# Four-layer diffusion transformer on one core: convolution taps dealt by head, and 32 modulation units of the third layer placed elsewhere

## The reference, cut to what matters

```
mod_x = silu(c) @ w_ada[i] + b_ada[i]          # 6 x 1024: shift1, scale1, gate1, shift2, scale2, gate2
```

```
s = q . k * scale (two maps per head) ;  p = softmax(s)
w = p[0] - lam * p[1] ;  attn = rmsnorm(w @ v)
z = a * sigmoid(g)                              # 512 channels
z = depthwise_conv(z, 31 taps) + b_dw ;  y_conv = silu(layernorm(z)) @ w_conv_out
out = (sigmoid(g1) * y_conv + sigmoid(g2) * (attn @ w_attn_out)) @ w_out
```

## Time and profile before

| | us |
|---|---|
| median of three runs | 2333.69 |
| lowest, highest | 2329.54, 2333.79 |
| the profiled execution's own time | 2330.94 |
| its span, first to last instruction | 2329.1 |
| TensorE busy | 2247.1 (96%) |
| VectorE busy | 1544.8 (66%) |
| ScalarE busy | 1082.7 (46%) |

### The profile page before, as it was taken

The page is one execution under the profiler, slowest core; times in us unless marked ns, Lnnn a source line. Parts: engine busy times, 40 slices in busy tenths (PEclk is TensorE's granted clock), DMA queues, the critical chain, the costliest instruction groups (busy, mean ns, idle before and its releaser), DMA issues.

```text
span 2329.1 us, 34905 instructions
## 1 busy us (share of the span) xinstructions
PE 2247.1 (96%) x13410; PEld 1869.9 (80%) x13410; DVE 1544.8 (66%) x2639; ACT 1082.7 (46%) x2070; POOL 33.4 (1%) x40
## 2 busy tenths in 40 slices
PE   8999999999899999989999999999999999989999
PEld 6658878888857898877777888888788887888988
DVE  5454777575656767578884455766754788767776
ACT  4453422223545555555566524422323765675543
POOL 0300000000100000000000000000000000000000
PEclk9999999999899999999999999999999999999999
DMA  8452467554365555311112232346652222254554
GB/s 315 159 191 73 154 213 268 178 181 135 107 238 181 195 179 174 105 58 61 46 55 73 75 116 73 138 157 212 216 182 91 91 91 75 80 163 148 192 185 138
DMA packets 95316, 335.44 MB, mean 144 GB/s; under 512 B 10672, under 2 KB 12848, under 8 KB 95024
## 3 DMA queue, kind: packets, MB, share of 16 engines
q1 hardware_dynamic: 95152, 333.21, 42.4%
HBM read 332.12 MB, written 1.05 MB: 143 GB/s over the span
## 4 chain that ended last, share of the span: by engine, by line
PE 81%; DVE 10%; ACT 5%; issue 3%; DMA 1%; SPq 0%; ACTq 0%; DVEq 0%
PE out L1507 19%; PE out L1509 19%; PE out L1508 19%; PE out L1501 7%; PE out L1505 3%; DVE w_lo L1909 2%; DVE stage L2270 2%; PE sc L1573 1%; PE pt L1582 1%; ACT w_hi L1639 1%; PE out L1434 1%; DMA raw<-stream 1%; ACT e_t L1802 1%; PE aux L1394 1%; PE pv L1598 1%
## 5 line engine op out<-in xcount | busy, mean ns | idle before, releaser
L1507 PE MATMUL out<-act,w_lo 128*128 128x512 f32 (+1 forms) x1816 | 648.4, 357 | 8.7 <-DVE w_lo L1909 2.9
L1639 ACT CAST w_hi<-raw 128x1024 fp32r<-128x1024 f32 (+2 forms) x444 | 453.8, 1024 | 431.3 <-PE out L1509 268.8
L1509 PE MATMUL out<-act,w_hi 128*128 128x512 f32 (+1 forms) x1816 | 637.4, 351 | 0.0
L1508 PE MATMUL out<-act,w_hi 128*128 128x512 f32 (+1 forms) x1816 | 637.0, 351 | 0.0
L1909 DVE TENSOR_TENSOR w_lo<-raw,w_hi 128x1024 fp32r<-128x1024 f32 (+2 forms) x444 | 528.3, 1192 | 123.0 <-ACT w_hi L1639 122.2
L1507 PEld LDWEIGHTS out<-act,w_lo 128*128 128x128 f32 x1816 | 345.2, 190 | 64.2 <-issue 12.9
L1509 PEld LDWEIGHTS out<-act,w_hi 128*128 128x128 f32 x1816 | 344.6, 190 | 45.9
L1508 PEld LDWEIGHTS out<-act,w_hi 128*128 128x128 f32 x1816 | 345.1, 190 | 43.5 <-issue 0.2
L1507 PE MATMUL out<-mix,w_lo 128*128 128x512 f32 (+1 forms) x734 | 261.5, 356 | 3.2 <-DVE mix L1931 2.2
L1508 PE MATMUL out<-mix,w_hi 128*128 128x512 f32 (+1 forms) x734 | 260.2, 354 | 0.0
L1509 PE MATMUL out<-mix,w_hi 128*128 128x512 f32 (+1 forms) x734 | 260.1, 354 | 0.0
(11 more groups left out here) (291 smaller groups left out, 2844.9 us busy)
## 6 DMA issues: line engine op xcount, KB each, us to landing
raw<-stream SPq DMA_DIRECT2D x604, 512.0 KB, 3.6
raw<-stream SPq DMA_DIRECT2D x16, 384.0 KB, 3.1
raw<-stream SPq DMA_DIRECT2D x16, 256.0 KB, 2.7
x<-xin SPq DMA_DIRECT2D x4, 512.0 KB, 5.3
consts<-const SPq DMA_DIRECT2D x1, 1088.0 KB, 7.1
x<-ctx SPq DMA_DIRECT2D x1, 1024.0 KB, 6.0
out<-x SPq DMA_DIRECT2D x8, 128.0 KB, 1.7
vecs<-vec SPq DMA_DIRECT2D x1, 287.0 KB, 9.0
```

The lines of the kernel that those rows point to most:

```text
L1507: nc.tensor.matmul(ps, wl, xh, start=(k == 0), stop=False)
L1508: nc.tensor.matmul(ps, wh, xl, start=False, stop=False)
L1509: ins = nc.tensor.matmul(ps, wh, xh, start=False, stop=(k == s.nk - 1))
L1639: nc.scalar.copy(w_hi[:, number % HL, 0:n], raw[:, place[number] % RAW, 0:n]).then_inc(S["hi_ready"], 1)
```

## The change

Three edits. The taps: `k_made` and `q_done` hold one tap each instead of three, and `taps_due` deals 24, 24, 6, 6, 6, 6, 6 to heads 0 to 6, evenly over a head's groups, and all that is left to head 7, in both the third and the fourth layer. The units: bank 1 of the third layer joins the first layer's network as `product`; bank 2 becomes 16 `ada` units in the third layer's mixer from head 2 on, one at the end of each group, in the bank `pt1`; the second layer's mixer has none. The last step of such a unit turns its result through a part of `stage` (`ada_turn`) instead of `k_t`.

```
-UNITS_IN = (1, 2, 2, 2, 2, 2)
+TAPS_IN = (24, 24, 6, 6, 6, 6, 6)
...
-        def taps_due(slots, head):
-
-            left = 4 * CONV_K - sum(taps_done) - 2 * 3 * max(0, 6 - head)
-            return max(0, -(-left // slots))
+        def taps_due(head, part, parts):
+
+            if head == 7:
+                return -(-(4 * CONV_K - sum(taps_done)) // (parts - part))
+            share = TAPS_IN[head]
+            return (part + 1) * share // parts - part * share // parts
...
-                qk_turn(held["k", h], lambda: conv_taps(3))
+                qk_turn(held["k", h], lambda: conv_taps(1))
...
-                held["qr", h] = query_finish(held["q", h], lambda: conv_taps(3))
+                held["qr", h] = query_finish(held["q", h], lambda: conv_taps(1))
...
             for j, g in enumerate(groups):
-                slots = (8 - h) * len(groups) - j
-                g.append(lambda slots=slots, h=h: conv_taps(taps_due(slots, h)))
-                for _ in range(UNITS_IN[j] if ada_left else 0):
-                    unit = ada_left.pop(0)
-                    g.append(lambda a=unit: ada(*a, psum="pt"))
-                    if unit[2:] == (1, KD - 1) or not ada_left:
-                        break
+                g.append(lambda h=h, j=j, parts=len(groups): conv_taps(taps_due(h, j, parts)))
+                if ada_left and h > 1:
+                    g.append(lambda a=ada_left.pop(0): ada(*a, psum="pt"))
...
-    seam = ffn(0, NT, mod_sums(1, [0, 1, 2]) + mod_sums(2, [0]), seam)
-    seam = layer_first(1, ada_list(2, [1, 2]), 3, seam=seam)
+    seam = ffn(0, NT, mod_sums(1, [0, 1, 2]) + mod_sums(2, [0, 1]), seam)
+    seam = layer_first(1, [], 0, seam=seam)
     seam = ffn(1, NX, [], seam)
-    seam = layer_second(2, seam)
+    seam = layer_second(2, seam, ada_list(2, [2]))
...
+        ada_turn = stage[:, 4336:4848]
...
-                    tr = k_t[:, 1, :]
+                    tr = ada_turn if s.psum == "pt" else k_t[:, 1, :]
```

## The result

The changed kernel takes 2337.0 us (median of 20 runs, 2331.22 to 2344.66), the kernel before in the same rounds 2333.64 us (20 runs, 2329.54 to 2342.4). The ratio is 1.0017 with a 95% interval of [1.001, 1.0024]: slower by 0.17%, just inside the 0.2% that I counted as no change. I had forecast 2325.1 us. The number lies in the range; the direction is wrong.

A forecast was written before the change was run, and what follows sets the result against it. TensorE, busy 2247.1 of 2329.1 us with 81% of the chain, was taken as the bound. Terms -15.7 + 2.8 + 8.5 + 1.5 - 3.7 + 0 - 2.0 = -8.6 us gave a median of 2325.1 us, range 2314 to 2341.

The forecast's parts named there:

- The two taps fewer in `q_done` and `k_made` are already in that: Third mixer, heads 0 and 1: the +8.5 us sum already credits the taps taken out of the two steps.
- Second mixer, -15.7: Second mixer's attention: taking out 32 units saves 15.7 us, bounds -7 and -21.3.
- rival 1: Second mixer: units were filler, their place becomes a wait; gain 7 instead of 15.7 us, 2333.8 us in all; chance 0.15.
- First network, +2.8: First network: 16 units as VectorE products and two more `modsum` steps cost 2.8 us, bounds +2.1 and +20.
- rival 3: First network: VectorE bounds it, costing +20 instead of +2.8 us, 2342 us in all; chance 0.08.
- Heads 0 and 1, +8.5 and +1.5: Third mixer: more taps lengthen the VectorE and ScalarE chain by 8.5 us, the clock adds 1.5; bounds +3 and +25.
- Rival 4: Third mixer, heads 0 and 1: taps fill idle VectorE time, costing 1 instead of 10 us; 2316 us in all; chance 0.15.
- Rival 2: Third mixer, heads 0 and 1: chain costs 25 instead of 10 us, with half-rate stretches; 2340 us in all; chance 0.12.
- The clock: Third mixer, heads 0 and 1: mean clock 0.96; more and longer waits add 1.5 us at half rate.
- Heads 2 to 6, -3.7: Third mixer: fewer taps close about 10.3 us of holes, units cost +0.7 and +7.6, clock -1.7; bounds -9 and +4.
- Head 7, 0 (to +4): Third mixer, head 7: 28 taps instead of 1 cost nothing, or up to 4 us if the layer norm's first sum is late.
- Fourth mixer, -2.0: Same tap deal: +0.8 us in heads 0 and 1, later heads lose 2.4 us of waits; bounds -3 and +5.

The follow-up runs named there:

- taps_after_n: Changed kernel, but in heads 0 and 1 the dealt taps stand only in groups behind the normalisation; 2356.84 us, ratio 1.0098 to the kernel before.
- after_again: The changed kernel run once more without any edit, for a second trace; 2338.28 us, ratio 1.0016 to the kernel before.
- units_only: Units moved as in the changed kernel, taps dealt as in the kernel before; 2323.47 us, ratio 0.9957 to the kernel before.
- taps_even: Changed kernel with dealt taps 14, 14, 12, 12, 12, 12, 12 in heads 0 to 6; 2333.67 us, ratio 1.0006 to the kernel before.
- prep3_after: Changed kernel with three taps instead of one in each preparation step, fewer at group ends, 26 in head 7; 2326.49 us, ratio 0.9965 to the kernel before.
- hidden_first: Changed kernel, but ScalarE makes the hidden tile's high part before the high part of later weights; 2336.14 us, ratio 1.0008 to the kernel before.
- prep5_even: Changed kernel with five taps in each preparation step, 16, 16, then 14 per head in all; 2317.87 us, ratio 0.9933 to the kernel before.

## Why the prediction was wrong

**The step that failed** stands in the part on heads 0 and 1, "The two taps fewer in `q_done` and `k_made` are already in that", and once more in the part on heads 2 to 6, "which shortens the chain by 1.4 to 2.8 us per item". Both count every tap at its duration of 0.71 us, wherever it stands. The four taps that left the two steps of each head had filled time in which VectorE waits for ScalarE: taking two out gave 0.25 us back in the query step and nothing in the key step, instead of 1.4. I had argued that place matters, and looked only at the place before the normalisation, which turned out not to matter (`taps_after_n`). With those taps put back, and all else of the change kept, the median is 2326.5 us; the forecast was 2325.1. That this is so near is partly luck, since other terms were off both ways, as follows.

Point by point:

- *Second mixer, -15.7*: -14.2 measured. A unit gave back 0.44 of its 0.55 us on the average, and rival 1 (the hole stays, 7 us) is out. But item by item the account was off. The item of the earlier trace rows, which was to fall from 5.69 to 4.9 us, fell to 5.46 only; the one before it fell from 6.56 to 4.54. In the changed kernel these two are:

```profile
686.23 1.13 PE L1572 MATMUL sc<-k_t,q_t 64*128 64x512 f32 x4
...
688.71 1.55 PE L1597 MATMUL pv<-p_t,v_t 128*64 128x128 f32 x16 [0.33 <-ACT p_t L1809]
...
690.77 1.13 PE L1572 MATMUL sc<-k_t,q_t 64*128 64x512 f32 x4
...
696.23 1.13 PE L1572 MATMUL sc<-k_t,q_t 64*128 64x512 f32 x4 [0.82 <-ACT e_t L1801]
```

  PV now waits 0.33 us for the copy, as expected. What I had not seen is the wait of the next S for the exponentials, 0.82 us. And the main wait of the stage is not for copies (1.1 us in three) but one of 1.9 us for the last item's normalisation. The granted clock stayed at 1.00 in this trace, with 8.8 us of holes in 60.1. It did not in `after_again`: behind the same wait of 1.9 us it fell to half rate, and the stage took 61.3 us. The Trainium skill ("TensorE: Matmul & The Clock Gate", section "Why this matters for your kernels") advises against long idle gaps between bursts of matmuls. Here one of 1.9 us was enough in some executions and not in others, at a cost of 1.3 us.
- *First network, +2.8*: right where nothing else happens (+2.3 to +2.7 in seven of the experiments, two of them with the swapped casts), but +5.8 in the changed kernel. VectorE was not the bound of the stage (238.63 of 294 us busy), so rival 3 is out, but at one place TensorE waits 1.9 us for VectorE's queue of products (1.4 us before), a backlog that I had called covered. The forecast's "I count that as hidden" for the stream failed at one place, by the late piece shown above. In the dense stretch from 310 to 324 us a piece lands 5.2 us after its issue in the changed kernel (median) and 4.0 us in `units_only`. Why the same list of steps gives one or the other is open: two executions of after, `taps_even` and `taps_after_n` lie at 394.0 to 394.7 us for this stage, `prep3_after` between (392.8 us, a wait of 2.7), the rest at 390.5 to 390.9.
- *Heads 0 and 1, +8.5 and +1.5*: +11.4, and 98.8 us where I said 97. T's waits are 11.6 us where I said 13. The size is nearly right for a partly wrong reason: the missing credit for the two steps is 3.6 us (`prep3_after`), which the covered items gave back. Rival 4 (the taps fill idle time, +1) is out for the taps at the ends of groups, and was right for those in the two steps. Rival 2 (25 us) is out.
- *The clock*: it fell to 0.91 from 0.96, as argued from the wait of 3.4 us, now up to 4.7. At 0.91, 2 x 0.09 x 98.9 = 18 us ran at 1.2 instead of 2.4 GHz, where it was 7 us before, though much of it in items that wait for VectorE anyway. `prep3_after` has the same 0.91 at 3.6 us less, so what the clock alone costs there isn't told apart.
- *Heads 2 to 6, -3.7*: -1.5, and -3.1 without a half-rate stretch (`hidden_first`). T's waits went from 11.6 to 2.9 us as forecast, and 16 units cost 5.7 to 7.3 us where I had +7.6 and +0.7 (14 x 0.55 is 7.7, a slip of no weight). The missing credit takes 1.9 us: with it (`prep3_after`) the stage is at -5.0.
- *Head 7, 0 (to +4)*: +2.0, of which the next row is the direct part, a wait of TensorE from 1256 to 1345 us for the last head's normalised output, behind 28 taps on VectorE.

```profile
PE aux L1605 <- DVE o_t L2249: 1.7, 1, 1.7
```

- *Fourth mixer, -2.0*: +0.4. Heads 0 and 1 +1.8 instead of +0.8, heads 2 to 6 -2.5 as forecast, and the last head +1.1 where I had put nothing. The same two steps lack their taps there; putting them back gives 1.7 us, 0.6 of it in heads 0 to 6 and 1.1 in the last head, which then also holds two taps fewer.

In sum, putting the taps back into the two steps takes 10.5 us off the median, of 11.9 us between forecast and result. About 6 us of that are shown in heads 0 to 6 as the place of the taps alone; up to 2.8 us lie in the last heads, where two taps fewer may do the same; the rest is within what half-rate stretches vary. The late piece adds 3.4 us, the second mixer's missing part 1.5. They add up to more than the miss because the rest of the chain in heads 0 and 1 was taken too large, by about 2 us (+7.8 with the credit, where I said +10.0).

## What to carry to other kernels

An engine's small fillers are worth their duration only in the closed loop; in a step where the engine waits for another anyway they are nearly free, so before moving them, look in the timeline at what follows them and whether it would start with a wait. Put as many fillers as fit into each such step, no more, and deal out the rest evenly. And when one change fills holes with work for the waiting engine and another closes the same holes, cost them together: one of the two gains is gone.

## What the runs showed that I had not expected

- *Work placed in an engine's queue behind an input that is late is held up, though it is ready.* With one cast queued behind a piece that ScalarE waited 8.15 us for, TensorE waited 3.69 us, and over five traces this wait grew with the piece's lateness. The swap of two calls was run only in traces in which the piece came earlier, so what it is worth when the piece is late isn't shown.
- *The clock's dips come and go.* Most half-rate stretches (3.4 to 10.2 us long) come with a wait of TensorE of 1.6 us or more, but the same wait has one in one execution and none in the next. The second mixer of the changed kernel has 8.8 us of holes; its last wait of 1.9 us was followed by a stretch in `after_again`, `taps_after_n` and `prep5_even` (61.3, 61.0 and 60.9 us), and not in the kernel after or in `units_only` (60.0). One stretch in the kernel before, at 1810 us, stands behind three waits of 0.4 to 0.6 us. Where TensorE is the bound, 3.4 us at half rate cost 1.6 to 1.7 us.
- *What a unit cost was not the same everywhere in one stage.* Taken out of the second mixer, the first 16 gave back more than the last 16 (about 7.3 to 8.2 against 6.0 us), and taking out all 32 gained between 0.1 and 4.4 us per item: a mean cost hides what the units had covered.
